# Norms from full-width column sums, a new spread of attention levels over the steps, and two output tiles on GpSimd

## The reference

```
def rms_norm(x, g):
    y = xf * lax.rsqrt(jnp.mean(xf * xf, axis=-1, keepdims=True) + EPS)
    return y * g
def modulated(x, mod, gains, j):
    return rms_norm(x, gains[j]) * (1.0 + mod[:, :, 3 * j + 1]) + mod[:, :, 3 * j]
def half_ffn(x, mod, gains, j, w_in, w_out):
    return x + FFN_RES * mod[:, :, 3 * j + 2] * swiglu(modulated(x, mod, gains, j), w_in, w_out)
```

## Time and profile before

| what | value |
|---|---|
| median of three runs | 1554.41 us (1553.52 to 1554.63) |
| the profiled execution | 1554.85 us, span 1553.2 us |
| busy: TensorE, VectorE, ScalarE, GpSimd | 1518.0, 1128.2, 661.7, 185.4 us |
| mean granted TensorE clock | 0.991 of full |
| ScalarE's copies for the high parts of weights (L1009) | 344.1 us |
| VectorE's subtractions for their low parts (L1482) | 403.3 us |

### The profile page before, as it was taken

How to read it: one execution, slowest core, us unless ns; L and a number is a source line. 1 busy time by engine, 2 the same in 40 slices (tenths; PEclk the granted TensorE clock), 3 DMA queues, 4 the chain that set the end, 5 groups by cost and what they waited for, 6 DMA issues and landing times.

```text
span 1553.2 us, 24614 instructions
## 1 busy us (share of the span) xinstructions
PE 1518.0 (98%) x8774; PEld 1479.9 (95%) x8774; DVE 1128.2 (73%) x1717; ACT 661.7 (43%) x956; POOL 185.4 (12%) x279
## 2 busy tenths in 40 slices
PE   9999999999979999999999999999989999999998
PEld 5999999989979999999999999998779999999998
DVE  5898888878987877688887777986977475444432
ACT  4433342369965433332343333325555454333321
POOL 0001000001240000001000000000794000000000
PEclk9999999999989999999999999999999999999999
DMA  9576676623423656677555666763222134334421
GB/s 384 185 253 216 230 242 218 201 68 108 151 96 109 213 183 194 198 228 232 171 179 186 191 189 214 250 196 113 68 82 77 61 109 149 122 128 141 152 93 41
DMA packets 68279, 257.04 MB, mean 165 GB/s; under 512 B 7584, under 2 KB 8608, under 8 KB 67968
## 3 DMA queue, kind: packets, MB, share of 16 engines
q1 hardware_dynamic: 48944, 187.57, 36.1%
q0 software_dynamic: 18512, 67.58, 13.5%
q10 hardware_dynamic: 768, 1.19, 0.2%
HBM read 253.68 MB, written 2.63 MB: 165 GB/s over the span
## 4 chain that ended last, share of the span: by engine, by line
PE 85%; DVE 7%; ACT 3%; POOL 2%; issue 1%; DMA 1%; SPq 0%; DVEq 0%; ACTq 0%; POOLq 0%
PE bank L557 26%; PE bank L559 25%; PE bank L558 25%; DVE tmp_a L1570 2%; DVE h_lo L1589 1%; DMA ada_first<-in_ada_w 1%; ACT w_hi_sb L1009 1%; PE wide L862 1%; DVE w_lo_sb L1482 1%; PE bank L656 1%; PE bank L570 1%; PE bank L884 0%; DVE bcum L2053 0%; ACT rgs L1261 0%; PE bank L901 0%
## 5 line engine op out<-in xcount | busy, mean ns | idle before, releaser
L1009 ACT ACTIVATE w_hi_sb<-raw 128x1024 fp32r<-128x1024 f32 (+3 forms) x308 | 344.1, 1122 | 477.3 <-PE bank L559 450.9
L557 PE MATMUL bank<-h_hi,w_hi_sb 128*128 128x384 f32 x1567 | 529.1, 338 | 2.3 <-ACT vt L1452 1.0
L1482 DVE TENSOR_TENSOR w_lo_sb<-raw,w_hi_sb 128x1024 fp32r<-128x1024 f32 (+3 forms) x308 | 403.3, 1310 | 170.3 <-ACT w_hi_sb L1009 167.0
L558 PE MATMUL bank<-h_lo,w_hi_sb 128*128 128x384 f32 x1567 | 526.6, 336 | 0.0
L559 PE MATMUL bank<-h_hi,w_lo_sb 128*128 128x384 f32 x1567 | 526.6, 336 | 0.0
L557 PEld LDWEIGHTS bank<-h_hi,w_hi_sb 128*128 128x128 f32 x1567 | 294.6, 188 | 6.4 <-DVE h_lo L1589 2.1
L558 PEld LDWEIGHTS bank<-h_lo,w_hi_sb 128*128 128x128 f32 x1567 | 294.6, 188 | 0.0
L559 PEld LDWEIGHTS bank<-h_hi,w_lo_sb 128*128 128x128 f32 x1567 | 294.6, 188 | 0.0
L557 PE MATMUL bank<-a_hi,w_hi_sb 128*128 128x384 f32 x704 | 236.8, 336 | 1.5 <-DVE a_lo L1704 1.5
L559 PE MATMUL bank<-a_hi,w_lo_sb 128*128 128x384 f32 x704 | 236.6, 336 | 0.0
L558 PE MATMUL bank<-a_lo,w_hi_sb 128*128 128x384 f32 x704 | 236.5, 336 | 0.0
(11 more groups left out here) (314 smaller groups left out, 1640.1 us busy)
## 6 DMA issues: line engine op xcount, KB each, us to landing
raw<-in_ffn_in SPq DMA_DIRECT2D x176, 512.0 KB, 3.8
ada_raw<-in_ada_w POOLq DMA_DIRECT2D x128, 512.0 KB, 3.7
raw<-in_ffn_out SPq DMA_DIRECT2D x64, 704.0 KB, 4.4
raw<-in_rg_in SPq DMA_DIRECT2D x20, 512.0 KB, 3.8
ada_first<-in_ada_w SPq DMA_DIRECT2D x8, 1024.0 KB, 19.1
raw<-in_rg_out SPq DMA_DIRECT2D x8, 640.0 KB, 3.9
raw<-in_gla_qk SPq DMA_DIRECT2D x8, 512.0 KB, 4.3
raw<-in_gla_v SPq DMA_DIRECT2D x8, 512.0 KB, 3.4
```

The costliest lines, as they stand in the source:

```text
L557: pe.matmul(out, w_hi_sb[:, slot, w], hi[k], start=start and j == 0, stop=False)
L558: pe.matmul(out, w_hi_sb[:, slot, w], lo[k], start=False, stop=False)
L1009: A(w_hi_sb[:, s, 0:w], raw[:, s, 0:w], ACT.Copy).then_inc(w_hi, 1)
L1482: V.tensor_tensor(w_lo_sb[:, s, 0:w], raw[:, s, 0:w], w_hi_sb[:, s, 0:w].bitcast(F32), ALU.subtract).then_inc(w_split, 1)
```

## The change

Three things change.

The norm: TensorE multiplies a full 128x128 matrix of ones with the squares (`column_sums`), so that the sums of all columns lie on all partitions at once, 256 sample columns in bank 6 and 128 prompt columns in bank 2. The reciprocal (VectorE) and then the root (ScalarE) are taken on these whole rows, samples first, into `scr[:, 3, :]`, which is now `rinv` and lies in SBUF. EPS enters with the first addition of squares. The spread is gone, the fillers are placed anew, and ScalarE's table load stands behind its first tile. In the opening the four partial sums go into TensorE without VectorE's third addition.

The attention: `LEVELS_AT` has other counts, one level in the first step for three.

The outputs: GpSimd makes output tiles 0 and 1 out of copies with gain that ScalarE prepares; VectorE makes the other six, and the stores have another order.

```diff
@@ -33,6 +33,7 @@
 EPS = 1e-6
+EPS_SUM = EPS * D / P
 N_MOD = 9
@@ -72,6 +73,9 @@
+Y_POOL = (0, 1)
+Y_DVE = [m for m in range(DC) if m not in Y_POOL]
+Y_ORDER = [2, 3, 0, 4, 5, 1, 6, 7]
 RING = 4
@@ -150,7 +154,7 @@
         ss, sq, sq_last = (scr[:, j, :] for j in range(3))
-        diag = scr[:, 3, :].rearrange("p (a b) -> p a b", a=NT)
+        rinv = scr[:, 3, :]
         rstd = sb("rstd", [P, HEADS * NT])
@@ -222,8 +226,7 @@
         bank += [ctx.enter_context(nc.psum_tensor(f"bank{i}", [P, 512], F32)) for i in (6, 7)]
-        sum_ps = bank[6][:, 0:NT]
-        rinv = bank[6][:, P:P + T]
+        col_sums = [bank[2], bank[6]]
@@ -396,7 +403,7 @@
         LEVELS_AT, n = [], 0
-        for count in (3, 2, 3, 2, 3, 2, 3, 2, 2, 2, 2, 2, 2, 2, 0, 0, 0):
+        for count in (1, 3, 3, 2, 2, 3, 2, 2, 2, 2, 3, 2, 2, 3, 0, 0, 0):
             LEVELS_AT.append(range(n, n + count))
@@ -470,8 +477,11 @@
-            for m in range(DC):
-                sp.wait_ge(h_ready, 8 * 6 + m + 1)
+            for m in Y_ORDER:
+                if m in Y_POOL:
+                    sp.wait_ge(y_on_pool, Y_POOL.index(m) + 1)
+                else:
+                    sp.wait_ge(h_ready, 8 * 6 + Y_DVE.index(m) + 1)
                 sp.dma_start(d["y"][:, m, :], y_out[:, m, :]).then_inc(out_done, 16)
@@ -547,6 +557,11 @@
+            for n, m in enumerate(Y_POOL):
+                pool.wait_ge(y_gained, n + 1)
+                pool.wait_ge(rinv_ready, 7)
+                nc.gpsimd.tensor_tensor(y_out[:, m, :], y_out[:, m, :], scr[:, 3, :], ALU.mult).then_inc(y_on_pool, 1)
 
@@ -569,45 +584,23 @@
-            def first_sums(q):
+            def column_sums(src, first=False, last=0):
+                for (t0, n, g), done in ((GROUPS[1], sum_part), (GROUPS[0], sum_done)):
+                    if last and src is sq_last:
+                        pe.wait_ge(sq_sample if g else sq_ready, last)
+                    mm = pe.matmul(col_sums[g][:, 0:n], ones[:, :], src[:, t0:t0 + n], start=first, stop=bool(last))
+                    if last:
+                        mm.then_inc(done, 1)
+            def norm(q):
                 pe.wait_ge(sq_added, (DC - 2) * (q + 1))
-                for t in range(NT):
-                    pe.matmul(sum_ps[:, t:t + 1], ss[:, t * P:(t + 1) * P], ones[:, 0:1], start=t == 0, stop=False)
-
-            def norm_sums(q):
-
-                if q:
-                    first_sums(q)
-                    keep_busy(2)
-                if q == 0:
-                    pe.wait_ge(sq_ready, 1)
-                    for t in range(NT):
-                        pe.matmul(sum_ps[:, t:t + 1], ss[:, t * P:(t + 1) * P], ones[:, 0:1], start=t == 0, stop=False)
-                else:
-                    pe.wait_ge(sq_sample, q)
-                for t in (1, 2, 0):
-                    if t == 0:
-                        pe.wait_ge(sq_ready, q + 1)
-                    last = pe.matmul(sum_ps[:, t:t + 1], sq_last[:, t * P:(t + 1) * P], ones[:, 0:1], start=False,
-                                     stop=t == 0)
-                last.then_inc(sum_done, 1)
-
-            def spread_factor(q):
-
-                pe.wait_ge(factor_ready, q + 1)
-                for t in range(NT):
-                    last = pe.matmul(rinv[:, t * P:(t + 1) * P], rstd[:, t:t + 1].to_broadcast([P, P]), ident,
-                                     start=True, stop=True)
-                last.then_inc(rinv_ready, 1)
-
-            def norm(q):
-
-                norm_sums(q)
-                keep_busy(3)
-                spread_factor(q)
+                column_sums(ss, first=True)
+                keep_busy(2)
+                column_sums(sq_last, last=q)
                 if q < 6:
-                    keep_busy(6)
+                    keep_busy(8)
@@ -691,10 +684,15 @@
                 turn_row(0)
-                keep_busy(8)
-                norm_sums(0)
+                keep_busy(4)
+                pe.wait_ge(sq_added, 3)
+                column_sums(tmp_a[:, 0, :], first=True)
+                column_sums(tmp_a[:, 1, :])
+                keep_busy(1)
+                pe.wait_ge(sq_added, 6)
+                column_sums(tmp_b[:, 0, :])
+                column_sums(tmp_b[:, 1, :], last=1)
                 turn_row(1)
-                spread_factor(0)
                 mod_row(2)
@@ -1019,11 +1017,13 @@
                 A(sq_last[:, 0:TP], x[:, DC - 1, 0:TP], ACT.Square).then_inc(sq_ready, 1)
-                norm_std(q)
-
-            def norm_std(q):
-                act.wait_ge(sum_done, q + 1)
-                A(rstd[:, 0:NT], sum_ps, ACT.Sqrt, bias=eps[:, :], scale=1.0 / D).then_inc(std_ready, 1)
+                norm_root(q)
+            def norm_root(q):
+                act.wait_ge(inv_part, q + 1)
+                A(rinv[:, TP:T], rinv[:, TP:T], ACT.Sqrt, scale=float(D)).then_inc(rinv_part, 1)
+                act.wait_ge(inv_ready, q + 1)
+                A(rinv[:, 0:TP], rinv[:, 0:TP], ACT.Sqrt, scale=float(D)).then_inc(rinv_ready, 1)
@@ -1066,7 +1066,7 @@
                 hi_of(1)
-                norm_std(0)
+                norm_root(0)
                 first_mods(0)
@@ -1092,11 +1092,12 @@
             def norm_apply(q, tables):
-                nc.scalar.preload_act_table_set(tables)
                 if q == 1:
...
                     high_h(q, m)
+                    if m == 0:
+                        nc.scalar.preload_act_table_set(tables)
                     if m == LATE:
@@ -1420,7 +1421,7 @@
                 if b >= DC - 2:
-                    level_exp(LEVELS_AT[0][b - DC + 3])
+                    level_exp(LEVELS_AT[1][b - DC + 2])
             for s in range(2 * DC):
@@ -1430,7 +1431,7 @@
                     key_factors(TURN_AT.index(s))
-                for n in LEVELS_AT[s + 1][:2]:
+                for n in LEVELS_AT[s + 1][:2] if s else ():
                     level_exp(n)
@@ -1465,6 +1466,8 @@
             only_weights("ffn_out3", 6, 2)
+            for m in Y_POOL:
+                A(y_out[:, m, :], x[:, m, :], ACT.Copy, scale=final_g[:, m:m + 1]).then_inc(y_gained, 1)
             norm_stats(6)
@@ -1529,8 +1532,10 @@
-                dve.wait_ge(std_ready, q + 1)
-                V.reciprocal(rstd[:, 0:NT], rstd[:, 0:NT]).then_inc(factor_ready, 1)
+                dve.wait_ge(sum_part, q + 1)
+                V.reciprocal(rinv[:, TP:T], col_sums[1][:, 0:TS]).then_inc(inv_part, 1)
+                dve.wait_ge(sum_done, q + 1)
+                V.reciprocal(rinv[:, 0:TP], col_sums[0][:, 0:TP]).then_inc(inv_ready, 1)
@@ -1547,9 +1552,10 @@
             def norm_apply(q):
-                dve.wait_ge(rinv_ready, q + 1)
                 if q == 6:
-                    for m in range(DC):
+                    dve.wait_ge(rinv_part, q + 1)
+                    dve.wait_ge(rinv_ready, q + 1)
+                    for m in Y_DVE:
                         V.scalar_tensor_tensor(y_out[:, m, :], x[:, m, :], final_g[:, m:m + 1], rinv,
@@ -1567,6 +1573,8 @@
                 for t0, n, g in GROUPS if m else reversed(GROUPS):
+                    if m == 0:
+                        dve.wait_ge(rinv_part if g else rinv_ready, q + 1)
                     last = V.scalar_tensor_tensor(tmp_a[:, m % 2, t0:t0 + n], x[:, m, t0:t0 + n],
@@ -1624,14 +1632,12 @@
                 dve.wait_ge(sq_made, 7)
-                V.tensor_tensor(tmp_b[:, :, :], tmp_b[:, :, :], first_sq[2], ALU.add).then_inc(sq_added, 3)
-                dve.wait_ge(sq_added, 6)
-                V.tensor_tensor(scr[:, 0:3:2, :], tmp_a[:, :, :], tmp_b[:, :, :], ALU.add).then_inc(sq_ready, 1)
+                V.scalar_tensor_tensor(tmp_b[:, :, :], tmp_b[:, :, :], EPS_SUM / 2, first_sq[2], ALU.add,
+                                       ALU.add).then_inc(sq_added, 3)
                 lo_of(0)
...
                 lo_of(2)
-                dve.wait_ge(rinv_ready, 1)
                 dve.wait_ge(gain_base, 1)
@@ -1722,7 +1728,8 @@
                     dve.wait_ge(sq_added, (DC - 2) * q + m - 1)
-                V.tensor_tensor(ss[:, :], ss[:, :], sq[:, :], ALU.add).then_inc(sq_added, 1)
+                V.scalar_tensor_tensor(ss[:, :], ss[:, :], EPS_SUM if m == 1 else 0.0, sq[:, :], ALU.add,
+                                       ALU.add).then_inc(sq_added, 1)
...
```

8 lines of the change are left out of this document (6 added, 2 removed).

## The result

The changed kernel takes 1570.0 us (median, 1568.8 to 1570.8) where the kernel before took 1554.5 beside it: ratio 1.0102, 95% interval 1.0089 to 1.0114, slower by 15.5 us. The forecast was 1562.0, with a range up to 1568. The direction was right and the size half of what came.

The account below looks back on a forecast made before the run. TensorE's feed-forward matmuls set the time; the change touches norms, opening, attention and tail. 5.1 + 1.0 + 1.2 + 2.4 - 4.0 + 1.9 = +7.6 on 1554.85 gives 1562.4, as a median 1562.0 us; range 1555.5 to 1568.

Parts of the forecast that it names:

- Reciprocals: Norms: VectorE's reciprocals take 1.75 us for 256 columns and 0.95 for 128, from the slope of narrow ones.
- The rival of cheap reciprocals: Norms: 256 columns cost what other operations cost, 0.42 us, so the kernel gets faster, 1546.8 us; chance 0.10.
- a third more per column: Seven norms: a wide reciprocal costs a third more per column than narrow ones, 0.8 us more each, 1567.6; chance 0.04.
- the +0.92: Inner norms: VectorE's scaling starts at 1267.10 in place of 1266.18 us, behind the two wide reciprocals.
- the table load's +0.1: Inner norms: the 1.28 us table load between ScalarE's first and second tile makes VectorE 0.1 us later.
- Small operations no longer hidden: First four norms: VectorE's biases, gain or half gate come on top, 0.1, 0.1, 0.3, 0.5 us; +1.0.
- The clock: Inner norms: one fall of TensorE's clock to half, in the norm at 1049, +1.2 us; bounds 0 and +6.
- The rival with falls in every norm (1568): The clock falls in every inner norm and once in the opening, four falls of 1.2 us and one more; chance 0.13.
- The opening: Start of kernel: reciprocals delay scaling, and the block matmul at 28.45 moves to 30.8 us; +2.4, bounds 0 and 3.5.
- Attention: Attention stage: the new level plan leaves 5.45 us of TensorE waits against 8.6; -4.0, bounds -8 and 0.
- The tail: Outputs: scaling 1.26 us later, two tiles fewer on VectorE -1.05, lockout with GpSimd +1.7; +1.9 in sum.

Follow-up runs that it names:

- a_open11: Changed kernel with eleven filler matmuls in TensorE's wait before the third modulation row of the opening; ratio to the kernel before 1.0109.
- a_open: Changed kernel with twenty filler matmuls in TensorE's wait before the third modulation row of the opening; ratio to the kernel before 1.0104.
- a_fill: Changed kernel with twelve more filler matmuls behind the sums of each inner norm; ratio to the kernel before 1.0086.
- c_ln_y8: Changed kernel with ScalarE's logarithm and exponential for reciprocal and root, and all eight output tiles on VectorE; 1550.0 us, ratio to the kernel before 0.9973.
- b_att_s11: Kernel before with only the new counts of levels, but two levels in step 10 and three in step 11; ratio to the kernel before 0.9986.
- a_lnexp: Changed kernel with ScalarE's logarithm and exponential in all seven norms for VectorE's reciprocal and the root; ratio to the kernel before 0.9999.

## Why the direction was right and the size was not

Three steps failed. The sum for the tail ended with VectorE's last tile and put what stands behind it at nothing more than before: the stores took 1.0 us more, and GpSimd's end of program 2.2. The waits of attention were taken as gained in full, -4.0 for -1.6. And the clock was counted in one norm, where it cost nothing, and not where it fell otherwise: three norms (1.6 to 1.8) and the gate steps (1.6). By terms:

- **Reciprocals: right.** 1.75 and 0.95 forecast, 1.757 and 0.894 measured. The two widths give (1757 - 894)/128 = 6.7 ns a column. The repeat count of 8 in the Trainium skill's "VectorE: DVE Perf Modes" (on the 8-slice pipeline), had it meant eight cycles a column, would have given 2.1 us for 256 (the forecast's estimate from that page); the measured 1.757 doesn't bear that reading out. The rival of cheap reciprocals is out, and so is that of a third more per column. Norm 5, with no fall of the clock, added 0.98 where 1.02 was forecast: both the +0.92 and the table load's +0.1 hold as a sum.
- **Small operations no longer hidden: right.** They show as 0.16, 0.14, 0.37 and 0.58 us, forecast 0.1, 0.1, 0.3 and 0.5. Less what the falls cost, norms 1 to 3 added 0.9 to 1.3 us each, forecast 1.1 to 1.3.
- **The clock: mis-sized.** I saw that TensorE would stand for 2.0 us, had no row between that and 2.54 us, and priced one fall at 1.2. Waits of 1.94 to 2.62 dropped it in four norms, 1.80 did not. Three cost 0.4 to 0.7 and the one I priced nothing: +1.7 for +1.2, near by luck, since the event that I priced and the events that cost are not the same. The rival with falls in every norm (1568) had the right event and a price twice too high. I never asked whether the clock would fall in places that the change only shifts: the one at 1189 costs 1.6, more than any in a norm. With a_open11's timing it doesn't come, so 1.6 of the 15.5 us hang on when that stretch comes.
- **The opening: right in sum.** +2.45 for +2.4; the scaling and the block matmul came within 0.6 us of the forecast. The first part didn't: 26.79 for 25.15, because of the row's wait and half clock, which I hadn't seen. The steps behind it took that up.
- **Attention: mis-sized, -1.6 for -4.0.** The waits of TensorE fell as forecast, 8.6 to about 5. I counted them as gained in full. The plan's own gain up to the gate steps is 2.5, since the value steps follow a chain of GpSimd and VectorE, and the moved levels cost 0.9 in the gate steps, where I had written "in later steps, where TensorE has no waits". Step 10 has one: three levels in a row need the merge of the first sooner. With the fall at 1189, norm 4 and attention came to +1.7 for -1.3.
- **The tail: the missed step is the end itself.** The scaling's start (behind norm 6's square it comes 1.39 us later than before, forecast 1.26), GpSimd's two tiles (2.26 us) and VectorE's 4.82 (forecast 4.94) were right. I ended the sum there. Two things stand behind it. From the scaling's start to SyncE's end it takes 7.99 us, 6.45 before: 0.5 of the 1.5 is VectorE's, the other 1.0 is in the stores. VectorE's first two tiles are late, so the stores bunch up: the last six follow each other without a pause from 1561.31, their issues take 0.43 to 0.46 us each for 0.33, and the last starts 0.76 us after VectorE's end, 0.03 before. Whether the slower issues come of the bunching or of something else isn't shown; every kernel here with tiles on GpSimd has them and none without. Then GpSimd's drain holds the program 2.2 longer. The drain was in the trace of before, 7.93 us after GpSimd's last operation at 1192.7, where it cost nothing. I followed only working instructions.

In sum: the clock in norms 1 to 3 1.6, norm 4 and attention with the fall at 1189 3.0, the tail 3.3.

## What to carry to other kernels

Before work is given to an engine that was finished, look at how its program ends: here GpSimd's drain needed 7.9 us behind its last operation, whatever that was, and work that it did later than that before the end was not free. A whole-row reciprocal on VectorE cost 6 to 7 ns a column here; where it stands on a latency path, take it of few columns, or take logarithm and exponential on ScalarE if the accuracy allows. Waits of TensorE in a stage that other engines pace are not gains to be collected: price a plan by that chain, and ask of each moved piece what it makes late.

## What the runs showed of the hardware

- GpSimd's drain at the end of a program ended 7.91 to 7.93 us after its last operation in all thirteen kernels, whether that was a tile of 384 columns, one of 192 or one column.
- In the norms of the changed kernel the granted clock was at half behind waits of TensorE of 1.94 to 2.62 us, and at full behind one of 1.80. No length of a wait divides the two: behind 2.02 us in a_open's norm 1 it stayed at full, and behind waits of 1.80 to 1.82 us in the value steps it fell in two kernels (near 1124 in a_fill, near 1114 in c_ln_y8) and not in two others (a_open11, b_att_s11). The stretch with one-column matmuls near 1189 us, with the same 0.54 us wait, fell in the changed kernel and not with the plan alone. What such a fall of 3.4 us cost ran from nothing (norm 4) to 1.6 us (gate steps).
- ScalarE's logarithm of 256 columns from PSUM took 0.38 us, its square or exponential of 256 from SBUF 0.42; of 128 columns 0.27 and 0.31 (a_lnexp). The source and the function differ together, so which of them makes the 0.04 us isn't shown.
